# A hybrid encoder layer: the MLP's first two hidden pairs activated later, and the last projection blocks reordered

## The reference

```
xn = RMSNorm(x); proj = xn @ w_in              # 1952 columns
group A: short conv, gates, long convolution   # 3 x 512 columns of proj
group B: latent attention, 8 heads             # q_lat 256, kv_lat 128, k_rope 32
x += concat(RMSNorm(A), RMSNorm(B)) @ w_out
h  = RMSNorm(x) @ w_mlp1                       # 1024 -> 4096
x += square(relu(h)) @ w_mlp2                  # 4096 -> 1024
x += sigmoid(x @ w_ple_gate) * RMSNorm(p @ w_ple_proj)
```

## Time and profile before

| what | value |
|---|---|
| time, median of 3 | 1848.68 us (1848.36 to 1849.76) |
| the profiled execution | 1849.01 us |
| its span (first to last instruction) | 1847.4 us |
| PE busy | 1765.0 us |
| DVE busy | 1328.7 us |
| ACT busy | 729.1 us |
| POOL busy | 402.9 us |
| mean granted clock of TensorE | 0.980 |

### The profile page before, as it was taken

One profiled execution on the slowest core, in us unless ns is written; L12 is line 12 of the kernel. 1 busy time (PEld: TensorE's weight loads), 2 busy tenths in 40 slices (PEclk: granted clock), 3 DMA queues, 4 the chain that ended last, 5 costly groups with the idle time before them and its releaser, 6 DMA issues.

```text
span 1847.4 us, 26440 instructions
## 1 busy us (share of the span) xinstructions
PE 1765.0 (96%) x10568; PEld 1598.3 (87%) x10568; DVE 1328.7 (72%) x1685; ACT 729.1 (39%) x1145; POOL 402.9 (22%) x256
## 2 busy tenths in 40 slices
PE   8999999988999998996899999999799999999999
PEld 6566788866899897885799999999699999999887
DVE  4695476855989988578655555556799898996634
ACT  6112221244777878135333333333333333333511
POOL 0000000002222220001122222212738384740000
PEclk9999999988999999998899999999899999999999
DMA  9223155032101012522232232226440312302021
GB/s 363 79 84 120 52 185 183 32 136 78 55 21 41 15 58 95 161 77 83 75 103 86 95 103 96 100 89 233 156 169 28 131 71 88 118 1 75 25 89 69
DMA packets 58461, 181.01 MB, mean 98 GB/s; under 512 B 6827, under 2 KB 7585, under 8 KB 57828
## 3 DMA queue, kind: packets, MB, share of 16 engines
q1 hardware_dynamic: 58340, 179.33, 27.7%
HBM read 135.96 MB, written 43.35 MB: 97 GB/s over the span
## 4 chain that ended last, share of the span: by engine, by line
PE 76%; DVE 14%; DMA 3%; ACT 3%; issue 3%; SPq 1%; POOL 0%; DVEq 0%; ACTq 0%; POOLq 0%
PE ps L3134 41%; PE ps L2614 18%; PE ps L2999 2%; PE ps L3027 2%; DVE ptl L2218 2%; PE ps L2673 2%; PE ps L3011 2%; DVE gmax L2175 2%; PE ps L2700 2%; PE ps L2712 1%; DVE K L1578 1%; PE ps L2661 1%; PE ps L2920 1%; DMA wst<-wb 1%; DVE wst L2131 1%
## 5 line engine op out<-in xcount | busy, mean ns | idle before, releaser
L3134 PE MATMUL ps<-rV,ringh 128*128 128x320 f32 x1248 | 237.0, 312 | 14.2 <-issue 14.1
L3134 PE MATMUL ps<-rU,ringh 128*128 128x320 f32 x1088 | 207.5, 313 | 12.4 <-DVE ringl L2385 9.6
L3134 PEld LDWEIGHTS ps<-rV,ringh 128*128 128x128 f32 x1248 | 198.1, 190 | 15.8 <-issue 15.8
L3134 PEld LDWEIGHTS ps<-rU,ringh 128*128 128x128 f32 x1088 | 173.4, 190 | 14.0 <-DVE ringl L2385 10.0
L2402 DVE TENSOR_TENSOR fH<-ps,fH 128x640 f32<-128x640 f32 x112 | 90.8, 823 | 126.0 <-PE ps L3134 126.0
L2614 PE MATMUL ps<-XL,wh 128*128 128x512 f32 x708 | 180.5, 364 | 0.0
L2614 PE MATMUL ps<-XH,wh 128*128 128x512 f32 (+1 forms) x612 | 166.3, 381 | 9.4 <-DVE wl L1555 2.8
L2614 PE MATMUL ps<-XH,wl 128*128 128x512 f32 (+1 forms) x612 | 155.9, 364 | 0.0
L3134 PE MATMUL ps<-rV,ringl 128*128 128x320 f32 x624 | 143.5, 311 | 0.0
L2614 PEld LDWEIGHTS ps<-XH,wh 128*128 128x128 f32 x612 | 105.8, 193 | 43.5 <-issue 21.6
L3134 PE MATMUL ps<-rH,ringh 128*128 128x320 f32 x736 | 138.9, 311 | 0.0
(11 more groups left out here) (400 smaller groups left out, 3900.1 us busy)
## 6 DMA issues: line engine op xcount, KB each, us to landing
hd<-fH SPq DMA_DIRECT2D x64, 320.0 KB, 2.3
wst<-wb SPq DMA_DIRECT2D x34, 512.0 KB, 3.4
wst<-wm SPq DMA_DIRECT2D x30, 512.0 KB, 3.8
fU<-hd SPq DMA_DIRECT2D x32, 320.0 KB, 3.8
w2b<-wm SPq DMA_DIRECT2D x16, 512.0 KB, 7.0
fH<-hd SPq DMA_DIRECT2D x24, 320.0 KB, 4.4
wraw<-wm SPq DMA_DIRECT2D x14, 512.0 KB, 3.7
xraw<-xT SPq DMA_DIRECT2D x8, 640.0 KB, 10.1
```

The source lines that it names most:

```text
L3134: ins = mm(out[:, c, :], a[:, w], two(b(xs[kk]))[:, c, :], start=kk == 0 and a is h and b is hi_of, stop=kk == 3 and a is l)
```

## The change

At the MLP's entrance:

- The norm's factor is no longer needed in product 2. The products of the first two rounds are added up unscaled, and their eight hidden parts and eight squares are held: `held_hidden(0)` and `held_hidden(1)` on the DVE at i = 13 and 14, the squares on ACT likewise. The tiles of both rounds stay in use until then.
- The factor goes another way: sums behind products 8 and 9, a transpose behind product 10 (`r_turn`), a copy to a row, a write to HBM and a read spread over all partitions into `dss`. The diagonal and the spread by PE are gone; the first twelve products use three PSUM slots (`THREE`).
- Squares: ACT squares x block 0 straight into `dss`, and blocks 1 to 4 behind the copies of the operands, not ahead of them. Blocks 5, 6 and 7 are squared later, from copies that SP loads back from HBM into H5, H6 and H7 (`late_x`). With them the order of the operands (`LOWS`), of the weights' splits and of SP's loads changes; the last `scale_x` comes in two halves.

At attention's entrance: `normed(13)` and `normed(14)` come earlier on the DVE; ACT takes tap 13 and two key squares ahead of the square of `latr`, and four key parts ahead of `krow`'s copy; the turn of the key scale comes behind the first eighth of block 15, not the second; SP writes and reads the key scale ahead of `store_gated(2)`; the query sums come in two halves behind eighths 5 and 6, and the second and third value tile behind the last one; the first scores wait only for `normed(14)`'s slot; the scaling of `tabq` comes behind two keys; taps 15 and `gate(3)` move to turns 4, 5 and 6.

The core of the diff (also in it: the same counts at the kernel's end, where the first square of the last norm goes straight to `dss`):

```
-        [(2, B11), (2, B21), (1, T4)], [(2, T3), (2, T2), (0, B22)],
-        [(3, B11), (3, T2), (3, B21), (2, T4), (3, T3), (1, T1), (2, T1), (3, T4), (3, T1), (1, B22), (2, B22), (3, B22)]]
+        [(2, B11), (2, B21), (1, T4)], [(2, T3), (2, T2), (3, B11)],
+        [(0, B22), (3, T2), (3, B21), (2, T4), (3, T3), (3, T4), (1, T1), (2, T1), (3, T1), (1, B22), (2, B22), (3, B22)]]
...
-            n = i % 3 if i < 6 else (i - 3) % 4
+            n = i % 3 if i < THREE else (i - THREE + 3) % 4
...
 SP
             store_gated(1)
+            sp.wait_ge(rows_ready, 2)
+            sp.dma_start(A["kid"].rearrange("h (t p) -> (h t) p", p=P), krow[:, :]).then_inc(rows_out, 16)
+            sp.wait_ge(rows_out, 32)
+            load_key_scale(0)
             store_gated(2)
...
-            sp.wait_ge(side_mm, 3)
+            sp.wait_ge(mm_done, J_MLA + KD)
+            for name, j in late_x:
+                m = MORD[j]
+                sp.wait_ge(x_in[m], 48)
+                sp.dma_start(raw(name), A["xd"][m]).then_inc(x_in[m], 16)
+            sp.wait_ge(n_sum, 4)
             load_w1(2)
+            load_w1(3)
+            load_w1(4)
+            load_w1(5)
+            sp.wait_ge(rows_ready, 5)
+            sp.dma_start(A["kvd"].rearrange("a (t p) -> (a t) p", p=P), rrow[:, :]).then_inc(rows_out, 16)
+            sp.wait_ge(rows_out, 80)
+            sp.wait_ge(side_mm, 1)
+            sp.dma_start(dss[:, :], A["kvd"].broadcast_to([P, T])).then_inc(r_in, 16)
...
 ACT
-            act.wait_ge(latr_in, 16)
-            fn(krsq[:, :], latr[:, :], ACT.Square).then_inc(kr_sq, 1)
             middle_tap(13)
-            for t in range(10):
+            for t in range(2):
+                key_square(t)
+            act.wait_ge(latr_in, 16)
+            fn(krsq[:, :], latr[:, :], ACT.Square).then_inc(kr_sq, 1)
+            for t in range(2, 10):
                 key_square(t)
...
             for j in range(KD):
+                if j == 7:
+                    weight_hi(1)
+                    weight_hi(2)
                 scale_x(j)
-                square_x(j)
+                if j == 6:
+                    weight_hi(0)
+                if j < 7:
+                    for kk, c in LOWS[j]:
+                        if kk < 3:
+                            first_hi(kk, c)
+                if j < 3:
+                    square_x(j)
+                elif 4 <= j < 6:
+                    square_x(j - 1)
                 if j in (1, 3):
                     split(B_OUT + 6 + j // 2, (mm_done, J_MLA + j + 1))
...
+                if i == 9:
+                    side_root(0, D)
+                if i == 10:
+                    act.wait_ge(turned, 5)
+                    fn(rrow[:, :], bank(6, P)[0:10, :], ACT.Copy).then_inc(rows_ready, 1)
+                if i in (13, 14):
+                    for at_, tile in enumerate(((parts[i - 13][1], 1), (parts[i - 13][0], 0), (parts[i - 13][1], 0),
+                                                (parts[i - 13][0], 1))):
+                        hidden_square(i - 13, at_ + 1, tile)
...
 DVE
-                if n == 0:
+                if n == 4:
                     left_tap(15)
-                if n == 1:
+                if n == 5:
                     right_tap(15)
-                if n == 2:
+                if n == 6:
                     gate(3)
...
+            def held_hidden(n):
+
+                a, b = parts[n]
+                dve.wait_ge(r_in, R_IN + 16)
+                for tile, h in (((b, 1), 0), ((a, 0), 0), ((b, 0), 1), ((a, 1), 1)):
+                    hidden_part(tile, h)
...
+            product_out(1)
             first_add(3, T4)
             first_add(3, T1)
+            weight_low(4)
+            add_square(4, (n_sq, 8 + 5))
+            late_square(5)
+            first_lo(3, T4)
+            product_out(2)
+            weight_low(5)
             first_lo(1, T1)
             first_lo(2, T1)
-            weight_low(3)
-            product_out(1)
-            first_lo(3, T4)
-            product_out(2)
-            weight_low(4)
-            dve.wait_ge(n_rt, 1)
-            diagonal(dsq)
             first_lo(3, T1)
+            product_out(3)
+            weight_low(6)
             for kk in range(1, 4):
                 first_lo(kk, B22)
-            product_out(3)
-            weight_low(5)
-            side_take(0, dss)
-            hidden_part((parts[0][1], 1), 0)
             product_out(4)
-            weight_low(6)
-            for i in range(4, 112):
+            weight_low(7)
+            late_square(6)
+            for i in range(5, 112):
...
 PE
-                if k == 1:
+                if k == 0:
                     key_scale_turn()
...
                 if k == 5:
                     value(0, 0)
+                    query_sums(0, range(5))
                 if k == 6:
-                    query_sums(0)
+                    query_sums(0, range(5, 10))
+                if k == 7:
                     value(0, 1)
                     value(0, 2)
...
-                if i == 1:
-                    side_sums(0)
-                if i in (2, 3):
-                    side_spread(0, i - 2)
+                if i in (8, 9):
+                    side_sums(0, range(5 * (i - 8), 5 * (i - 8) + 5))
+                if i == 10:
+                    r_turn()
```

More of the change, by code:

```diff
@@ L55 @@
 NPROD = 16 * 7 + 4 * 28
+THREE = 12
 B_PLE = B_MLP + NPROD
@@ L777, in _ @@
                 a, b = parts[n % 2]
-                if 2 * n + 3 < 32:
+                if 1 < n and 2 * n + 3 < 32:
                     load_w1(2 * n + 3)
@@ L796, in _ @@
                 store_hidden(n, 1, (b, 1), 0, 2 * n)
-                if 2 * n + 4 < 32:
+                if 0 < n and 2 * n + 4 < 32:
                     load_w1(2 * n + 4)
@@ L1028, in _ @@
             fn(kroot[:, :], kroot[:, :], ACT.Sqrt, bias=par("eps"), scale=1.0 / QK).then_inc(kss_ev, 1)
+            for q in range(2):
+                key_part(q)
             act.wait_ge(kr_t, 1)
             fn(cshift[64:96, :], kroped[96:128, :], ACT.Copy).then_inc(kr_u, 1)
-            for q in range(6):
+            for q in range(2, 4):
                 key_part(q)
@@ L1035, in _ @@
             fn(krow[:, :], bank(0, P)[0:80, :], ACT.Copy).then_inc(rows_ready, 1)
+            for q in range(4, 6):
+                key_part(q)
             fn(kroped[96:128, :], kroped[64:96, :], ACT.Copy).then_inc(kr_u, 1)
@@ L1333, in _ @@
                     first_product_out(n)
-                weight_hi(i + 3)
-                if q == 3:
+                if i > 3:
+                    weight_hi(i + 3)
+                if i == 9:
[7 more added lines that the diff above has]
+                        hidden_square(i - 13, at_ + 1, tile)
+                if n > 1 and q == 3:
                     hidden_square(n, 1, (b, 1))
-                if q == 5:
+                if n > 1 and q == 5:
                     hidden_square(n, 2, (a, 0))
-                if q == 6:
+                if n > 1 and q == 6:
                     hidden_square(n, 3, (b, 0))
-                if q == 0:
+                if n > 2 and q == 0:
                     hidden_square(n - 1, 4, (parts[(n - 1) % 2][0], 1))
@@ L2041, in _ @@
             right_tap(12)
+            normed(13)
             dve.wait_ge(wk_hi, 1)
@@ L2059, in _ @@
             gate(0)
-            normed(13)
             lows(15)
@@ L2199, in _ @@
             key(0, 1)
+            dve.wait_ge(tabq_in, 16)
+            scale(tabq[:, :], tabq[:, :], par("q_norm"))
+            st.settle()
             value_lo(0, 0)
@@ L2529, in _ @@
                 weight_low(i + 3)
+                if i == 6:
+                    late_square(7)
+                if i == 10:
+                    dve.wait_ge(n_rt, 1)
+                    V.reciprocal(rinv[:, 0:10], root[:, 0:10]).then_inc(diag_ready, 1)
+                if i == 13:
+                    held_hidden(0)
+                if i == 14:
+                    held_hidden(1)
                 if i in (109, 110):
```

154 lines of the change are left out of this document (87 added, 67 removed).

## The result

The changed kernel takes 1824.43 us (median of four runs, 1823.06 to 1825.09) beside 1848.52 for the kernel before on the same chip: a ratio of 0.987 (95% interval 0.9855 to 0.9886), 24 us or 1.3% less. The prediction said 1821, 1810 to 1834. The profiled execution has a span of 1823.2 us and a mean clock of 0.989.

A forecast was written before the change was run, and what follows sets the result against it. PE, busy 96% of the span, was taken to bound the kernel, with time to win at two thin entrances. Attention -9.4 and MLP -18.8 sum to -28.2 us, from 1849.0 to 1820.8, said as 1821, range 1810 to 1834.

The forecast's parts named there:

- step 5: Attention, turn 9: weights queued behind the moved `gate(3)` come late; PE waits 5.2 us plus 3.0 half clock, bounds 0 to 11.
- Step 1: Attention's entrance, block 14: the 3.49 us wait and the half clock behind it go; block 15 starts at 391.2, minus 8.5.
- Steps 2 to 4: Attention, block 15 to first turn: first scores at 426.9 against 444.97, first turn at 433.2 against 450.79, minus 17.6 us.
- step 2: Attention, block 15: piece 8 still waits 2.5 us but comes 0.9 sooner, at 405.0, minus 9.4.
- R1: Rival, attention's turn 9: the wait does not arise, through a faster load or ScalarE's slack; 1812.6 us, chance 0.14.
- Step 6: MLP's entrance up to residual 6: the DVE loses square sums and waits, gains others; 857.11 becomes about 856.2.
- Step 7: MLP's entrance behind residual 6: the DVE's queue, 36.5 us with 4.5 for GpSimd, decides; product 7 at 892.7 against 914.0.
- Step 8: MLP, products 7 to 12: factor's sums and turn lie behind product 7, spread gone; product 12 at 912.8, not 931.6.
- Step 9: MLP, held hidden parts and squares: factor there at about 917.5, 9 us to spare, so the hold costs nothing.
- R4: Rival, MLP's product 17: the hold delays its low weights if the factor comes 37 us late; 1852 at 40, chance 0.03.
- R2: Rival, MLP's entrance: DVE loses GpSimd's full time, PE's clock stays low between products 0 and 6; 1829, chance 0.14.
- R3: Rival, either entrance: one gives nothing, its waits only move; 1830 for attention, 1840 for the MLP, chance 0.07.

The follow-up runs named there:

- parts_first: Changed kernel with ScalarE's order in block 15 edited: key part 6 ahead of tap 14, part 7 behind the tap; 1823.06 us, ratio 0.9874 to the kernel before.
- att_only: Kernel before with only attention's part of the change, the MLP as before; 1837.63 us, ratio 0.9953 to the kernel before.
- weights_first: Changed kernel with SP loading weights `B_ATT + 2` ahead of the last gated tile's store and key scale 2; 1817.82 us, ratio 0.9835 to the kernel before.
- gate_early: Changed kernel with taps 15 and `gate(3)` back in turns 0, 1 and 2; 1816.88 us, ratio 0.984 to the kernel before.
- hi_first: Changed kernel with ScalarE copying high halves of weight 0 and part 2's T3 and T2 ahead of `scale_x(6)`; 1820.96 us, ratio 0.9855 to the kernel before.
- sums_later: Changed kernel with GpSimd's second pair of round 1 weight sums behind weight 8's low half, not weight 6's; 1820.84 us, ratio 0.9864 to the kernel before.
- pool_small: Changed kernel with GpSimd's sums for rounds 0 and 1 cut from 512 columns to 16, not computing the layer; 1814.56 us, ratio 0.9826 to the kernel before.
- mlp_only: Kernel before with only the MLP's part of the change, attention's entrance as before; 1829.55 us, ratio 0.990 to the kernel before.
- factor_late: Changed kernel with SP writing the factor's row ten times more before its read, `load_w1(6)` moved ahead; 1829.58 us, ratio 0.9904 to the kernel before.
- four: Changed kernel with the edits of `parts_first`, `weights_first` and `hi_first`, and tap 15 on ScalarE behind the first exponential; 1816.53 us, ratio 0.9846 to the kernel before.

## Why the prediction was right, and where its sizes were off

The forecast (faster, 1821) was off by 3.4 us and right by its own mechanism: two entrances that give their gains apart, the DVE deciding in the second. Its terms were less exact: attention's gain up to turn 0 was 3.3 us too large and the MLP's 2.0, and step 5's cost, 1.0 too large, made up for a part of that.

- **Step 1.** Right in place, too large in size. The 3.49 went, but a new wait of 3.70 came, with the lower clock behind it. From the first key token to block 15 were 23.4 us before; 15.0 were forecast, 17.2 came in the profiled execution, and 15.9 to 18.4 in the twelve traces with attention's changed entrance. Block 15 started at 393.49 in the profiled execution, against 391.2 forecast. In the twelve traces it started between 389.29 and 394.19 (mean 391.6); the mean meets the forecast only because the first key token stood up to 2.8 sooner than before in several of them (373.4, against 376.2), which the prediction did not count on. The prediction did not see that the first key token then waits for `LL` (up to 3.7).
- **Steps 2 to 4.** Piece 8 waits 2.47, as said. From block 15 to turn 0 were 43.04 us, and 42.9 to 43.1 in the ten traces without the edit of `parts_first`; the prediction's times give 42.0 (433.2 less 391.2). Half of the 1.0 is missing ahead of the first scores (36.17 against 35.7), half in the chain behind them (6.87 against 6.3). `parts_first` shows that step 2's wait covers another behind it.
- **Step 5.** Right mechanism, term too large: 8.2 forecast, 6.0 in the profiled execution, 4.2 over the traces. ScalarE's wait was 7.93 (7 said), but PE's only 3.63. Turn 9 stood 40.5 behind turn 0, 3.1 later than before (37.4), and not 42.6: `query_sums(1)`, and with it `gate(3)`, ran 28.3 behind turn 0 (464.87) and not 29.9, since the waits of the first turns were gone, and the weights were there 4.3 behind their issue and not 4.7. The half clock behind the wait was sized right: turn 9 to turn 10 took 6.93 in place of 4.13, 2.8 against 3. In five of the seven traces with this step and the queue unchanged PE's wait at turn 9 was only 2.0 to 2.3, because the lower clock had come before it, behind the wait of 2.14 that the moved steps put into turn 7, and PE was late itself: so it was in `att_only`, where turn 8 took 1.91 and turn 9 1.10. R1 (nothing there) is wrong. `weights_first` keeps the step and `gate_early` undoes it, and they end alike (348.68 and 347.87), so the step pays for nothing: the short waits that it removes cost 3.2, those that it adds in turns 4 to 8 are 2.5 (0.35 and 2.14).
- **Attention, sum.** Forecast -9.4 (-17.6 at turn 0, then 8.2 lost); -7.1 at the last wait in the profiled execution (-14.3 at turn 0, then 7.2 lost), and 0.47% or 8.7 us by `att_only`.
- **Step 6.** Residual 6 at 848.88, which is 855.9 with attention's 7.06 put back; 856.2 said. First product 860.2 (860.3 said).
- **Step 7.** The DVE decides, shown by `hi_first` and `sums_later`. Product 7 at 894.8 in the same reckoning, against 892.7. The GpSimd term was sized 4.5 and measured 5.70 (`pool_small`); about 1 us more is in the chain of the last T2 (1.5, with 1.2 said), in short gaps of 0.1 to 0.2 between other operations, and between the low half's end and product 7. By the Trainium skill (SBUF — State Buffer, two separate sides) the prediction weighed 9.2, priced by GpSimd's rows (1.30 and 1.75 to a pair). The runs show what was wrong in that pricing: a row of 1.75 holds GpSimd's own waiting, since the same sum takes 1.30 in `sums_later`. Blocking by 1.3 at most for each of the six sums, 7.8 in all, leaves room for the measured 5.7, so the trace does not speak against the rule.
- **Step 8.** 20.0 us from product 7 to product 12, 20.1 said. MLP: -16.8 at product 12 (-18.8 said), 0.99 of the time before by `mlp_only`, 17.1 us.
- **Step 9.** The hold costs nothing and 9 us are to spare: `factor_late` shows 9.2. R4 is a real mechanism with the right place (the low half of weight 17), far from deciding.

R2 and R3 did not occur: the clock was 0.92 in the MLP's entrance, GpSimd's share 5.7 and not 9.2, and each entrance gave its own part.

Open: why the loads of block 14 are issued and land up to 3 us apart from one execution to another, with which the first key token moves by as much (373.4 to 376.3 in the twelve traces), and why the stretch near 345 us runs at the lower clock in some executions and not in others. No experiment tried that.

## What to carry to other kernels

When a step is moved to a later place, look at what is queued behind its transfers, not only at its own engine: here a load of 256 KB standing behind a store cost 4 to 7 us, and moving that one line ahead of the store gave them back. In a stretch where one engine decides, each us taken from its queue is won at the stretch's end (1.97 of 2.02 in `hi_first`) until the next engine is reached (1.81 of 2.18 in `sums_later`), so add up its queue; where a wait is taken away and two operations were due at about the same time, look for the second before pricing it. Compare kernels by intervals between marks in the traces, and see first which of them repeat: from the last wait of attention to product 7 six kernels with the same code there had 97.29 to 97.32, while from turn 0 to that wait seven had 350.75 to 353.92, and the four times of the changed kernel lay 2 us apart.

## What the runs showed of the hardware

- A 128x512 sum on GpSimd takes 1.30 us alone and 1.73 to 1.91 beside the DVE's low halves; for each sum the DVE lost up to 1.1 (1.0 at 885.58, where GpSimd began first and kept its 1.30); two of these with two sums took 3.73 in place of 1.55. Beside the DVE's `fH<-ps,fH`, which reads PSUM, neither lost anything (1.55 for two, as alone, and GpSimd 1.30, at 884 us in `sums_later`). The Trainium skill (SBUF — State Buffer, two separate sides) says this of a DVE operation with two operands in SBUF, and the rows agree.
- Ten dependent writes of a 5 KB row took 1.3 us each in `factor_late` (13.07 in all), while the first one with its wait had taken 2.05 (901.06 to 903.11).
- In `four` the table load of 1.28 us on ScalarE started at 432.32, only when the row maximum that the exponential behind it needs was there, after 3.82 us in which ScalarE stood: it was not hidden behind that wait.
